# RMS-norm factors of a two-layer diffusion backbone on one Trainium2 core: sums in four strips of 32 columns, root and Newton step on a quarter of the columns, and one product that spreads the factors

## The reference

```
def rms_norm(x, g):
    xf = x.astype(jnp.float32)
    y = xf * lax.rsqrt(jnp.mean(xf * xf, axis=-1, keepdims=True) + RMS_EPS)
    return (y * g.astype(jnp.float32)).astype(x.dtype)

def modulate(h, shift, scale):
    return h * (1.0 + scale) + shift

    hl = modulate(rms_norm(xl, norm1_g[l]), ml[:, :, 0], ml[:, :, 1])    # norm 1 of a layer
    hl2 = modulate(rms_norm(xl, norm2_g[l]), ml[:, :, 3], ml[:, :, 4])   # norm 2 of a layer
```

## Time and profile before

| | us |
|---|---|
| median of 3 runs | 1653.53 |
| the runs | 1650.42 to 1655.39 |
| the profiled execution's own time | 1656.43 |
| its span, first to last instruction | 1654.8 |
| PE busy in the span | 1485.0 (90%) |
| DVE busy | 861.9 (52%) |
| ACT busy | 629.1 (38%) |
| POOL busy | 368.4 (22%) |
| mean granted PE clock | 0.947 of full speed |

### The profile page before, as it was taken

One profiled execution on the slowest core, in us unless ns is written; L12 is line 12 of the kernel. 1 busy time (PEld: TensorE's weight loads), 2 busy tenths in 40 slices (PEclk: granted clock), 3 DMA queues, 4 the chain that ended last, 5 costly groups with the idle time before them and its releaser, 6 DMA issues. The chain is left out here.

```text
span 1654.8 us, 19911 instructions
## 1 busy us (share of the span) xinstructions
PE 1485.0 (90%) x7944; PEld 1079.3 (65%) x7944; DVE 861.9 (52%) x1252; ACT 629.1 (38%) x838; POOL 368.4 (22%) x196
## 2 busy tenths in 40 slices
PE   6998998889999998789999996899979997998887
PEld 2565677657777776478888873597958996333334
DVE  4711576683132334699998984745583565211112
ACT  2422221174132223468778763442245443010102
POOL 0322331102223231010101002174304662000000
PEclk9899999789999999799999997899979997999998
DMA  9457321003666551489999994143313577899993
GB/s 342 131 184 272 108 77 51 27 20 128 208 204 213 188 184 51 158 313 412 406 403 404 409 360 152 51 141 114 108 40 128 207 237 279 323 421 420 421 421 160
DMA packets 118029, 367.27 MB, mean 222 GB/s; under 512 B 8046, under 2 KB 73776, under 8 KB 86960
## 3 DMA queue, kind: packets, MB, share of 16 engines
q1 hardware_dynamic: 109168, 334.58, 54.0%
q0 software_dynamic: 8768, 31.40, 5.1%
HBM read 353.37 MB, written 12.58 MB: 221 GB/s over the span
## 5 line engine op out<-in xcount | busy, mean ns | idle before, releaser
L760 POOL TENSOR_TENSOR w_lo<-ring,w_hi 128x1024 fp32r<-128x1024 f32 x120 | 301.5, 2520 | 600.8 <-ACT w_hi L1671 600.6
L896 PE MATMUL bank<-h_hi,w_hi 128*128 128x512 f32 (+1 forms) x768 | 271.9, 354 | 8.2 <-DVE h_lo L2020 6.3
L897 PE MATMUL bank<-h_hi,w_lo 128*128 128x512 f32 (+1 forms) x768 | 264.7, 345 | 0.0
L898 PE MATMUL bank<-h_lo,w_hi 128*128 128x512 f32 (+1 forms) x768 | 264.6, 344 | 0.0
L896 PEld LDWEIGHTS bank<-h_hi,w_hi 128*128 128x128 f32 x768 | 148.0, 193 | 51.3 <-issue 28.8
L898 PEld LDWEIGHTS bank<-h_lo,w_hi 128*128 128x128 f32 x768 | 148.1, 193 | 17.2
L897 PEld LDWEIGHTS bank<-h_hi,w_lo 128*128 128x128 f32 x768 | 148.3, 193 | 16.7 <-issue 1.2
L896 PE MATMUL bank<-w_hi,h_hi 128*128 128x512 f32 (+1 forms) x384 | 141.6, 369 | 10.2 <-DVE w_lo L2360 5.1
L898 PE MATMUL bank<-w_lo,h_hi 128*128 128x512 f32 (+1 forms) x384 | 138.0, 359 | 0.0
L897 PE MATMUL bank<-w_hi,h_lo 128*128 128x512 f32 (+1 forms) x384 | 137.9, 359 | 0.0
L1671 ACT ACTIVATE w_hi<-ring 128x1024 fp32r<-128x1024 f32 x120 | 125.3, 1053 | 31.3 <-PE bank L896 18.4
(11 more groups left out here) (339 smaller groups left out, 2798.4 us busy)
## 6 DMA issues: line engine op xcount, KB each, us to landing
ring<-in_w_in SPq DMA_DIRECT2D x52, 1024.0 KB, 5.1
ring<-in_w_down_e SPq DMA_DIRECT2D x36, 1024.0 KB
ring<-in_w_up_e SPq DMA_DIRECT2D x34, 1024.0 KB, 7.9
mix<-in_w_gate_e SPq DMA_DIRECT2D x32, 1024.0 KB, 7.8
operands_plain<-in_w_gate_e SPq DMA_DIRECT2D x29, 1024.0 KB, 23.4
ring<-in_w_mod SPq DMA_DIRECT2D x24, 1024.0 KB, 7.0
mix<-in_w_mod SPq DMA_DIRECT2D x24, 1024.0 KB, 4.9
mix<-in_w_up_e SPq DMA_DIRECT2D x22, 1024.0 KB, 23.5
```

The costliest lines, as they stand in the source:

```text
L760: pool.tensor_tensor(w_lo[:, slot], rview(raw, 8)[:, :, x * P:(x + 1) * P], w_hi[:, slot].bitcast(F32), ALU.subtract).then_inc(w_l, 1)
L896: first = mm(dst, stat[0], mov[0], start=start, stop=False)
L897: mm(dst, stat[1], mov[0], start=False, stop=False)
L898: return first, mm(dst, stat[0], mov[1], start=False, stop=stop)
```

## The change

- The sums of norms 0 to 3 are made in four strips. Each call of `norm_sum` issues four products, each with a matrix of ones of 32 columns on one quarter of the token columns, into one group of 32 partitions of the bank. The mean, the root and the first two Newton instructions then work on 128 columns (64 in norm 3) in place of 512 (256).
- The third Newton instruction becomes four, one for each strip, each on a single partition (0, 32, 64, 96), written to its own place in a buffer `strips` that is otherwise zero. A new product `norm_spread` of the 128x128 ones with `strips` puts the factors back into all partitions and all columns, in a PSUM bank. The scaling of the stream reads that bank.
- `strips` is cleared before each norm by a memset on DVE: in front of norm 0's root, at tile 5 of each output product, and in front of the residual adds of L2650.
- Norms 1 and 3: DVE no longer adds squares. PE does the sum of block m-2 behind tile m of the output product (from tile 2 on), and the last two behind the loop.
- Norm 2: PE does the sum of block k-3 behind the transposes of block k (from block 3 on), and the last three behind the loop, with the spreading product behind them and ahead of the filter products.
- Norm 0: the spreading product stands behind L954, ahead of the last two modulation steps.

```diff
@@ buffers
-        nrm = area(18432 + 1024, 2048).rearrange("p (i t) -> p i t", i=4)
+        nrm = area(18432 + 1024, 1536).rearrange("p (i t) -> p i t", i=3)
+        strips = area(18432 + 1024 + 1536, 512)
+        def spread_bank(inst):
+            return bank[4 if inst % 2 else 1]
@@ PE
             def norm_sum(inst, cols, k):
                 pe.wait_ge(n_sq, inst * DK + k + 1)
-                mm(norm_bank(inst)[:, 0:cols], ones, sqb[:, k % 2, 0:cols], start=k == 0, stop=k == DK - 1
-                   ).then_inc(n_mm, 1)
-
-            def norm_sum_added(inst, cols):
-                pe.wait_ge(n_ad, inst // 2 + 1)
-                mm(norm_bank(inst)[:, 0:cols], ones, nrm[:, 1, 0:cols], start=True, stop=True).then_inc(n_mm, 1)
+                w = cols // 4
+                for c in range(4):
+                    last = mm(norm_bank(inst)[32 * c:32 * c + 32, 0:w], ones[:, 0:32],
+                              sqb[:, k % 2, c * w:(c + 1) * w], start=k == 0, stop=k == DK - 1)
+                last.then_inc(n_mm, 1)
+
+            def norm_spread(inst, cols):
+                pe.wait_ge(n_r, inst + 1)
+                mm(spread_bank(inst)[:, 0:cols], ones, strips[:, 0:cols], start=True, stop=True).then_inc(n_b, 1)
@@ PE, start
                     elif k == 5:
                         spectra_a(l, 0)
+                        if l == 0:
+                            norm_spread(0, NT)
@@ PE, layer 1
                 if l:
-                    for k in range(DK):
+                    for k in range(DK - 3, DK):
                         norm_sum(2 * l, NT, k)
+                    norm_spread(2 * l, NT)
                     pe.wait_ge(z_x[l - 1], 16 * l)
                     filters(l, 1)
@@ PE, output product, tile m
                     if l == 0 and m == 2:
                         mod_columns(1, 2)
+                    if m >= 2:
+                        norm_sum(2 * l + 1, T, m - 2)
                 pe.wait_ge(o_pe[l], DK * l + DK)
                 pe.nop().then_inc(w_u, 1)
 
-                norm_sum_added(2 * l + 1, T)
+                for k in range(DK - 2, DK):
+                    norm_sum(2 * l + 1, T, k)
+                norm_spread(2 * l + 1, T)
@@ PE, transposes of block k
                     last.then_inc(z_t[l], 1)
+                    if k >= 3:
+                        norm_sum(2 * l + 2, NT, k - 3)
@@ ACT
-                A(nrm[:, 2, 0:cols], nrm[:, 0, 0:cols], ACT.Abs_reciprocal_sqrt).then_inc(n_s, 1)
+                A(nrm[:, 2, 0:cols // 4], nrm[:, 0, 0:cols // 4], ACT.Abs_reciprocal_sqrt).then_inc(n_s, 1)
@@ DVE
             def norm_dve_root(inst, cols):
                 norm_dve_mean(inst, cols)
+                w = cols // 4
+                mean, root, tmp = nrm[:, 0, 0:w], nrm[:, 2, 0:w], nrm[:, 1, 0:w]
                 dve.wait_ge(n_s, inst + 1)
 
-                link(V.tensor_tensor(nrm[:, 3, 0:cols], nrm[:, 2, 0:cols], nrm[:, 2, 0:cols], ALU.mult))
-                link(V.scalar_tensor_tensor(nrm[:, 3, 0:cols], nrm[:, 0, 0:cols], -0.5, nrm[:, 3, 0:cols],
-                                            ALU.mult, ALU.mult))
-                link(V.scalar_tensor_tensor(nrm[:, 1, 0:cols], nrm[:, 3, 0:cols], 1.5, nrm[:, 2, 0:cols],
-                                            ALU.add, ALU.mult))
+                link(V.tensor_tensor(tmp, root, root, ALU.mult))
+                link(V.scalar_tensor_tensor(tmp, mean, -0.5, tmp, ALU.mult, ALU.mult))
+                for c in range(4):
+                    row = slice(32 * c, 32 * c + 1)
+                    last = V.scalar_tensor_tensor(strips[row, c * w:(c + 1) * w], tmp[row], 1.5, root[row], ALU.add, ALU.mult)
+                last.then_inc(n_r, 1)
+
+            def clear_strips():
+                link(V.memset(strips, 0.0))
 
             def norm_dve_scale(inst, cols):
                 hT = hTs[inst]
+                spread = spread_bank(inst)[:, 0:cols]
+                dve.wait_ge(n_b, inst + 1)
...
-                            V.tensor_tensor(hT[:, k, 0:cols], xT[:, k, 0:cols], nrm[:, 1, 0:cols], ALU.mult
+                            V.tensor_tensor(hT[:, k, 0:cols], xT[:, k, 0:cols], spread, ALU.mult
@@ DVE, output product, tile m
+                    if m == 5:
+                        clear_strips()
                     if l + 1 < DEPTH and m in (1, 4):
                         angle(l + 1, m // 4)
-                    if m >= 3:
-                        squares_added(m - 2)
                 dve.wait_ge(o_d[l], 16 * l + 8 * S)
-                for k in range(DK - 2, DK):
-                    squares_added(k)
                 norm_dve(2 * l + 1, T)
```

More of the change, by code:

```diff
@@ L359, in build @@
         n_mm = sem("norm_sums")
-        n_ad = sem("norm_squares_added")
         n_a = sem("norm_mean")
         n_s = sem("norm_root")
+        n_r = sem("norm_factors_in_strips")
+        n_b = sem("norm_factors_spread")
         n_x = sem("norm_scaled")
@@ L1973, in norm_dve_mean @@
             def norm_dve_mean(inst, cols):
+                w = cols // 4
                 dve.wait_ge(n_mm, (inst + 1) * DK)
-                V.tensor_scalar(nrm[:, 0, 0:cols], norm_bank(inst)[:, 0:cols], 1.0 / D, EPS, ALU.mult, ALU.add).then_inc(n_a, 1)
+                V.tensor_scalar(nrm[:, 0, 0:w], norm_bank(inst)[:, 0:w], 1.0 / D, EPS, ALU.mult, ALU.add).then_inc(n_a, 1)
             def norm_dve_root(inst, cols):
                 norm_dve_mean(inst, cols)
+                w = cols // 4
+                mean, root, tmp = nrm[:, 0, 0:w], nrm[:, 2, 0:w], nrm[:, 1, 0:w]
                 dve.wait_ge(n_s, inst + 1)
-                link(V.tensor_tensor(nrm[:, 3, 0:cols], nrm[:, 2, 0:cols], nrm[:, 2, 0:cols], ALU.mult))
-                link(V.scalar_tensor_tensor(nrm[:, 3, 0:cols], nrm[:, 0, 0:cols], -0.5, nrm[:, 3, 0:cols],
-                                            ALU.mult, ALU.mult))
-                link(V.scalar_tensor_tensor(nrm[:, 1, 0:cols], nrm[:, 3, 0:cols], 1.5, nrm[:, 2, 0:cols],
-                                            ALU.add, ALU.mult))
+                link(V.tensor_tensor(tmp, root, root, ALU.mult))
[6 more added lines that the diff above has]
+                link(V.memset(strips, 0.0))
             def norm_dve_scale(inst, cols):
                 hT = hTs[inst]
+                spread = spread_bank(inst)[:, 0:cols]
+                dve.wait_ge(n_b, inst + 1)
                 if inst == 1:
@@ L2323, in _ @@
                 trail_merged(DK - 1)
-                def squares_added(k):
-                    inst = 2 * l + 1
-                    total = nrm[:, 1, 0:T]
-                    dve.wait_ge(n_sq, inst * DK + k + 1)
-                    if k > 1:
-                        dve.wait_ge(n_mm, inst * DK + k)
-                    add = V.tensor_tensor(total, sqb[:, 0, 0:T] if k == 1 else total, sqb[:, k % 2, 0:T], ALU.add)
-                    if k == DK - 1:
-                        add.then_inc(n_ad, 1)
-                    else:
-                        add.then_inc(n_mm, 2 if k == 1 else 1)
                 for m in range(DK):
```

## The result

The changed kernel takes 1661.82 us (median of 6 runs, 1656.91 to 1668.8), the kernel before 1654.46 on the same chip. One of the six executions of the kernel before took 1749.06 us, far off all others, and the ratio goes by the rest. The ratio is 1.0064, with a 95% interval of 1.0047 to 1.0082: slower by 0.64%, 10.6 us (7.8 to 13.6). By the medians the difference is 7.4 us, or 8.3 without that execution, so 10.6 is the high reading of a loss that lies nearer to 8. I had forecast 1652.3 and a range up to 1658.5. The profiled execution of the changed kernel took 1668.8 us (span 1667.1), the longest of its six, so a stage's length is better evidence than its end.

A forecast was written before the change was run, and what follows sets the result against it. The end was taken as set by when layer 1's expert-weight loads resume, behind all four norms. Terms 0.85 - 0.2 - 3.4 + 1.6 = -1.2 us gave 1655.2 profiled, 1652.3 as median; range 1647.5 to 1658.5.

The forecast's parts named there:

- +0.85 us. The faster sums buy nothing: Norm 0: PE waits for modulation weights anyway; the spreading product ahead of the last two modulation steps costs 0.84 us.
- twice that, at 1.2 GHz: Norm 0: upper bound for the spreading product's cost, twice 0.84 us, if PE ran at 1.2 GHz.
- Norm 1: Layer 0's output product: -2.5 us behind it, +2.3 us from five strip sums inside it, net -0.2.
- Norm 2: Sums ride between the transposes, so scaling starts at 1045.5 in place of 1049.03: -3.4 us after rounding down.
- Norm 3: Layer 1's output product: -0.2 us behind it, +1.8 us from five sums inside it, +1.6 in all.
- the rival that the loads hide norm 3: Layer 1's weight loads set the end by volume, swallowing norm 3's +1.6: 1650.7 us; with the forecast, chance 0.77.
- The strips do run side by side: Rival denied this in output products and norm 2's transposes: calls of 1.09 and 0.67 us, +5.6, 1659.1; chance 0.08.
- The clock did not stay up at the router product: Rival claimed PE's clock holds at the router products behind norms 1 and 3: -5.5 us, 1648.0; chance 0.14.
- Reading the bank costs nothing: Scaling: factors read from a bank in place of the local buffer priced at nothing; from above under 1 us per norm.
- The four pieces of the last Newton instruction: On DVE: starts taken 0.32 us apart for 128 columns, the dearer choice; 0.21 kept for the range.

The follow-up runs named there:

- six fillers: Six idle products in PE's gap ahead of the fourth modulation step; with only norm 0 changed 0.9981, -3.1 us against the kernel before.
- norm 2 alone: Changed kernel with norms 0, 1 and 3 put back as before, run twice against the kernel before: 0.9983 (-2.8 us) and 0.9973 (-4.5 us).
- norm 3 alone: Changed kernel with norms 0, 1 and 2 put back as before, run twice against the kernel before: 1.0024 (+4.0 us) and 1.0012 (+2.0 us).
- the one with the rare loop: Only norm 3 changed, its six strip sums inside the output product left out; an expert exceeded its capacity and the loop for that ran: 4267.85 us.
- norm 0 alone: Changed kernel with norms 1 to 3 put back as before, against the kernel before: 1.0022, +3.6 us; with six idle products 0.9981, -3.1 us.
- the whole with fillers: All four norms changed, six idle products in PE's gap ahead of the fourth modulation step: 1.0026, +4.3 us against the kernel before; an earlier comparison gave 1.0038.
- the kernels of parts: Changed kernel with the old code put back for some norms; alone, norm 0 gave +3.6 us, norm 1 +0.5, norm 2 -2.8 and -4.5, norm 3 +4.0 and +2.0.
- the two that leave sums out: Only norm 1 or only norm 3 changed, the six strip sums inside its output product left out: 0.9990 (-1.7 us against the kernel before) and 4267.85 us.
- the three with one to three products in the gap: Spreading product moved into PE's gap, all norms changed: 1.0036; two idle products, norm 0 changed: 1.0002; two plus spreading product, norms 0 and 2 changed: 1.0017.

## Why the prediction was wrong

**The step that failed is norm 0, "+0.85 us. The faster sums buy nothing", with its bounds "from below nothing, from above twice that".** The first half was right: the sums bought nothing, PE waited for the load. The wait was priced as free, and the clock behind it was left out. I had the row of that wait before me (1.58 us at 26.71) and treated more of it as free. The runs put +3.6 us (1.2 to 6.3) in its place, 5.4 to 6.4 inside the whole change, and six products that do nothing take 3.8 to 6.7 us off. I had even priced the clock for one event, "twice that, at 1.2 GHz" for the spreading product, where I had to ask which work stands behind the longer pause: filter products and three modulation steps, on the path. In the profiled executions the split is complete. All seven of kernels with the new norm 0 and fewer than six fillers have filter products of 7.19 us, behind idle times (the one just ahead of the fourth step) of 1.83 to 6.58 us; the 1.83 has the 2.66 ahead of it. All thirteen others (nine with the old norm 0, four with six fillers) have 3.70, behind 0.28 to 2.26. This term does not carry the whole miss: the forecast was -1.2 us, and what else is missing stands under the open points.

**Norm 1: right in the terms that count.** The root ends 2.3 us behind the last residual add, as written; the stretch to the router product shrinks by 2.51 us (predicted 2.5). PE nowhere waits for a square between the tiles. The spreading product takes 1.93 us where I had 1.12, but ACT's splits hide it. Inside the product five sums cost 2.63 us (from the second add to the last, 37.39 us in place of 34.76), 0.53 a call where I took 0.46. The net is +0.1 in the trace, +0.5 in the run, predicted -0.2.

**Norm 2: right in sign; that the size agrees is partly luck.** Its two runs gave -2.8 and -4.5 us for my -3.4. In the trace the gain at the scaling is only 1.8 to 2.0. Two terms were mis-sized. The spreading product takes 2.08 us where I had 1.12: PE waits 3.06 us ahead of it, and it runs at half clock. And the sums push the residual adds by more than the 0.4 us that I gave them: from the first add's start to the last one's end it takes 7.84 us (8.03 in the changed kernel's trace) in place of 6.64, with DVE waiting 0.76 us for the fifth block's transposes, which stand behind the first sum and take 1.12 us (0.66 for the next ones). The scaling then starts 6.36 us behind the last add, not 5.6. The filter products don't start where they did, but 1.7 us later, counted from the first add. They take 7.19 us in place of 3.70, and the first projection product, which waited 4.27 us for DVE with the old norm 2, now follows them at once.

From the first residual add to the 25th record of L919 in the projections it takes 46.16 us with the new norm 2 alone (second run), where a kernel with the old norm 2 (norm 3 alone, second run) takes 48.65: 2.5 us gained. But the old norm 2 has a better case than that. In six of its nine profiled executions the granted clock is down for part of the first 5 us behind the first add (0.57 to 0.71 on average), and they take 48.1 to 48.8 us; in the three others it is at full there, and they take 46.5. All eleven with the new norm 2 have the clock down there, and ten of them take 46.2 to 46.4 (one 45.5). So the gain is 2 to 2.5 us with the clock down and a few tenths against the better case; whether the new one would gain in that case too, no execution shows. First the new norm 2, then the old:

```profile
1029.26 3.37 DVE L2706 SCALAR_TENSOR_TENSOR xT<-bank,mods,xT 128x256 f32<-128x256 f32 x8 [0.16 <-PE bank L1562]
1033.38 3.72 DVE L2706 SCALAR_TENSOR_TENSOR xT<-bank,mods,xT 128x256 f32<-128x256 f32 x8 [0.76 <-PE bank L1562]
...
1043.35 7.19 PE L963 MATMUL bank<-mix 64*128 64x512 f32 x8
1050.47 0.58 PE L917 MATMUL bank<-h_hi,w_hi 128*128 128x256 f32 x1
...
1075.42 0.28 PE L919 MATMUL bank<-h_lo,w_hi 128*128 128x256 f32 x1
```

```profile
1027.28 6.64 DVE L2706 SCALAR_TENSOR_TENSOR xT<-bank,mods,xT 128x256 f32<-128x256 f32 x16 [0.82 <-PE bank L1562]
...
1039.71 3.70 PE L963 MATMUL bank<-mix 64*128 64x512 f32 x8
1047.68 0.55 PE L917 MATMUL bank<-h_hi,w_hi 128*128 128x256 f32 x1 [4.27 <-DVE h_lo L2069]
...
1075.93 0.28 PE L919 MATMUL bank<-h_lo,w_hi 128*128 128x256 f32 x1
```

The last stage asks for the same care. From the first product L1270 behind layer 1's router (L1301 there) to the end it takes 255.0 us in both profiled executions of norm 2 alone, where all other kernels of this case (the one with the rare loop apart) take 257.4 to 260.0, others with the new norm 2 among them. Nothing of norm 2 stands there, so about 3 us of the gain have a cause that no run shows.

**Norm 3: right in sign, too small.** Five sums cost 2.2 us, 0.43 each, where I had 0.36 and 1.8. Behind the product I had -0.2 at the scaling. It is -0.06 in the first trace of the changed kernel, but +0.3 in its two later traces and in both runs of norm 3 alone, where the spreading product takes 1.22 us in place of my 0.70. With 0.4 us for the slower router product, 2.2 + 0.3 + 0.4 = 2.9 us in the trace of norm 3 alone. The runs gave +4.0 and +2.0 for my +1.6. They also speak against the rival that the loads hide norm 3.

**The rivals.** The strips do run side by side: a call costs 0.43 to 0.53, not the "about 1 us" at which that rival decides. The clock did not stay up at the router product (9.41 us); I had that rival on the faster side only, and the same mechanism in the other direction, at norm 0, decided the case. Reading the bank costs nothing, as I took it: eight scalings take 2.74 us (2.77 before). The four pieces of the last Newton instruction take 1.17 us, 0.29 apart with 0.28 for each, nearer to the 0.32 that I took than to the 0.21 of the earlier trace rows. The Trainium skill, "VectorE: DVE Perf Modes", section "Two Vector instructions with no wait between them", says that an instruction whose output begins in another group of 32 partitions starts only when the earlier ones have finished. The trace agrees with it.

**What stays open.** The parts, +3.6, +0.5, -3.7 (mean of two) and +3.0 (mean of two), sum to +3.4 us; the whole gave +7.1, +8.1 and +10.6. Each part is uncertain by about 2 us, so 4 to 5 us of difference could be chance, but no run explains it, and the fillers gained less in the whole (3.8) than in norm 0 alone (6.7). The granted clock doesn't look like the reason for what they leave: the whole with fillers is 4.3 us slower than the kernel before though its mean clock is not lower (0.9512 and 0.9503). The traces show where time is lost. From the router product of layer 0 to the first residual add of norm 2 all six profiled executions with four norms changed take 368.2 to 369.4 us, the kernel before 366.5, the kernels of parts (without the two that leave sums out) 365.6 to 368.2. Norm 1 is over there and norm 2 not begun, so I had priced nothing in that stage, and why it is 2 to 3 us longer stays open.

## What to carry to other kernels

Making an engine faster ahead of a wait that does not move only makes the wait longer; on PE ask what stands behind that pause, since it may run at half clock, and price that work twice. Before an idle time is called free, look for rows in which the same engine came out of a pause of that length, and see what its next products took. When a change has several parts, measure each by itself: here the one that shortens a chain which others wait for (norm 2) gained, and the one that inserts work into a product without a gap (norm 3) lost.

## What was not expected of the hardware

One pause at the start was followed by a long slow stretch: in the seven profiled executions with the clock down, the granted clock stood at half for 13.7 to 20.5 us on end, though PE worked nearly without a break from the fourth step on. In the three with one to three products in the gap the clock fell all the same; with six it held, in four of four.

Reading the factor from a bank changed a stall. In the kernel before, the first two scalings of norm 0 took 3.43 us while POOL split weights; in the changed kernel, also beside POOL, they take 1.27, and the next instruction, which reads no bank, takes 1.32 in place of 0.40:

```profile
56.40 1.27 DVE L2033 TENSOR_TENSOR mix<-xT,bank 128x512 f32<-128x512 f32 x2
57.60 1.32 DVE L2038 TENSOR_SCALAR mix<-mix,gs,mods 128x256 f32<-128x256 f32 x1
```

The stage of three instructions is 1.2 us shorter for it (48.88 to 52.63 us before, 56.40 to 58.92 now). It is so in all eleven profiled executions with the new norm 0, and the old 3.43 and 0.40 stand in all nine with the old one. No run changes the bank alone, so that it is the reason is only my reading.
